# GpSimd's sums and differences written in pieces of half the width or less

## What is computed

```python
        x = x + jnp.einsum('bse,ed->bsd', mixed, w_out[l])
        h = rmsnorm(x, norm_mlp[l])
        u = jax.nn.relu(jnp.einsum('bsd,df->bsf', h, w_up[l]))
        x = x + jnp.einsum('bsf,fd->bsd', u * u, w_down[l])
```

## Time and profile before

| | |
|---|---|
| median of three timed runs | 2396.8 us (2395.7 to 2396.91) |
| the profiled execution | 2394.05 us, of which the span is 2392.4 us |
| TensorE matmul busy | 2326.6 us, 97% |
| VectorE busy | 1520.1 us, 64% |
| ScalarE busy | 1154.1 us, 48% |
| GpSimd busy | 706.9 us, 30%, 593 instructions |

### The profile page before, as it was taken

One profiled execution on the slowest core, in us unless ns is written; L12 is line 12 of the kernel. 1 busy time (PEld: TensorE's weight loads), 2 busy tenths in 40 slices (PEclk: granted clock), 3 DMA queues, 4 the chain that ended last, 5 costly groups with the idle time before them and its releaser, 6 DMA issues.

```text
span 2392.4 us, 34959 instructions
## 1 busy us (share of the span) xinstructions
PE 2326.6 (97%) x11346; PEld 1934.7 (81%) x11346; DVE 1520.1 (64%) x2623; ACT 1154.1 (48%) x2226; POOL 706.9 (30%) x593
## 2 busy tenths in 40 slices
PE   7999999999999998999899999999999999999998
PEld 5888888788888886887687877888888888888887
DVE  6588873688888886566745655444465555564454
ACT  5211112788888886223545555555553233333243
POOL 2000000111111114235568764666640032120132
PEclk9999999999999999999999999999999999999999
DMA  5567765666666565766455576654457486564464
GB/s 189 215 235 278 268 242 163 180 160 156 160 157 157 152 156 169 248 218 202 170 183 163 189 286 242 202 160 152 154 190 260 165 298 234 193 219 162 138 219 160
DMA packets 253970, 469.09 MB, mean 196 GB/s; under 512 B 59336, under 2 KB 119752, under 8 KB 246032
## 3 DMA queue, kind: packets, MB, share of 16 engines
q1 hardware_dynamic: 247808, 451.11, 58.6%
q0 software_dynamic: 6048, 16.52, 2.6%
HBM read 316.13 MB, written 151.42 MB: 195 GB/s over the span
## 4 chain that ended last, share of the span: by engine, by line
PE 51%; DVE 3%; POOL 2%; issue 2%; DMA 1%; ACT 1%; SPq 0%; POOLq 0%; ACTq 0%; DVEq 0%
PE m_ps L2533 24%; PE m_ps L2556 23%; PE m_ps L1685 4%; DMA b_kept<-f_kept 1%; POOL m_mix L1548 1%; DVE f_up_lo L2389 1%; PE m_ps L2574 0%; DVE m_xn L1653 0%; DVE m_xm L1646 0%; DVE m_mix L1622 0%; ACT m_mix_hi L1585 0%; DVE keep_lo L2408 0%; POOL h_raw L1560 0%; POOL f_kept L2157 0%; DVE hop_lo L1659 0%
## 5 line engine op out<-in xcount | busy, mean ns | idle before, releaser
L2556 PE MATMUL m_ps<-keep_hi,hop_hi 128*128 128x512 f32 x880 | 342.5, 389 | 0.4 <-DVE hop_lo L2392 0.4
L2556 PE MATMUL m_ps<-keep_hi,hop_lo 128*128 128x512 f32 x880 | 342.4, 389 | 0.0
L2556 PE MATMUL m_ps<-keep_lo,hop_hi 128*128 128x512 f32 x880 | 342.3, 389 | 0.0
L2392 DVE TENSOR_TENSOR hop_lo<-h_raw,hop_hi 128x512 fp32r<-128x512 f32 x224 | 176.6, 789 | 236.8 <-ACT hop_hi L2228 236.7
L2389 DVE TENSOR_TENSOR f_up_lo<-wide_raw,f_up_hi 128x512 fp32r<-128x512 f32 x160 | 182.5, 1142 | 223.0 <-ACT f_up_hi L2223 222.9
L2228 ACT ACTIVATE hop_hi<-h_raw 128x512 fp32r<-128x512 f32 x224 | 140.8, 630 | 334.4 <-PE m_ps L2556 330.5
L958 POOL DMA_DIRECT2D o_main<-a_o x63 | 36.5, 580 | 775.2 <-ACT a_o L1326 726.6
L599 PE MATMUL p_ps_o<-p_ht_lo,p_w_hi 128*128 128x512 f32 x576 | 224.5, 390 | 0.0
L2533 PE MATMUL m_ps<-keep_hi,f_up_hi 128*128 128x512 f32 x512 | 202.8, 396 | 6.1 <-DVE f_up_lo L2389 4.7
L2533 PE MATMUL m_ps<-keep_hi,f_up_lo 128*128 128x512 f32 x512 | 201.3, 393 | 0.0
L2533 PE MATMUL m_ps<-keep_lo,f_up_hi 128*128 128x512 f32 x512 | 199.4, 390 | 0.0
(11 more groups left out here) (246 smaller groups left out, 5779.8 us busy)
## 6 DMA issues: line engine op xcount, KB each, us to landing
h_raw<-u_ops SPq DMA_DIRECT2D x224, 256.0 KB, 4.2
wide_raw<-in_w_up SPq DMA_DIRECT2D x32, 1024.0 KB, 7.2
u_ops<-f_u SPq DMA_DIRECT2D x128, 256.0 KB, 4.3
wide_raw<-in_x SPq DMA_DIRECT2D x59, 512.0 KB, 4.0
u_ops<-f_us SPq DMA_DIRECT2D x96, 256.0 KB, 2.3
proj_hi<-p_o_hi SPq DMA_DIRECT2D x17, 1024.0 KB, 6.2
proj_lo<-p_o_lo SPq DMA_DIRECT2D x17, 1024.0 KB, 8.3
h_raw<-in_w_down SPq DMA_DIRECT2D x58, 256.0 KB, 3.9
```

The source lines that it names most:

```text
L2392: nc.vector.tensor_tensor(lo, a_raw[:, (m - UP) % A_RING], hi.bitcast(F32), ALU.subtract).then_inc(op_lo_done, 1)
L2556: last = nc.tensor.matmul(down_banks[b % 2][t][:], a[:, cols], w[j], start=(j == 0 and m == 0), stop=(j == FG - 1 and m == 2))
```

## The change

The operations and their operands stay. Those of 512 columns become two of 256, L1560 with 1024 columns becomes two of 512, L2143 with 1024 becomes four of 256, and L2128 with 2048 becomes eight of 256. Waits stand ahead of the first piece, and the last piece signals. In numbers: 6 more instructions at L1560, 128 in `mix_w`, 128 in `mix_u`, 7 in `mix_tokens`, 24 in `mix_rest`, 293 in all.

```diff
@@ mix_out: mix_tokens
-                nc.gpsimd.tensor_tensor(dst[:, k], a[:, k], b[:, k], ALU.subtract).then_inc(t_mixed, 1)
+                for m in range(k.start, k.stop):
+                    last = nc.gpsimd.tensor_tensor(dst[:, m], a[:, m], b[:, m], ALU.subtract)
+                last.then_inc(t_mixed, 1)
...
+    def combine(dst, a, b, op):
+
+        half = dst.shape[1] // 2
+        for cols in (slice(0, half), slice(half, 2 * half)):
+            last = nc.gpsimd.tensor_tensor(dst[:, cols], a[:, cols], b[:, cols], op)
+        return last
...
@@ mix_w, mix_u: eight lines of this form
-                nc.gpsimd.tensor_tensor(s1[:], a21, a22, ALU.add).then_inc(w_mixed, 1)
+                combine(s1[:], a21, a22, ALU.add).then_inc(w_mixed, 1)
...
@@ mix_tokens
-            nc.gpsimd.tensor_tensor(raw[:, 2], raw[:, 2], raw[:, 0], ALU.subtract).then_inc(t_mixed, 1)
+            for k in range(4):
+                last = combine(raw[:, 2, k], raw[:, 2, k], raw[:, 0, k], ALU.subtract)
+            last.then_inc(t_mixed, 1)
...
@@ mix_rest
-            nc.gpsimd.tensor_tensor(dst[:, k], a[:, k], b[:, k], ALU.subtract).then_inc(t_mixed, 1)
+            for m in range(k.start, k.stop):
+                last = combine(dst[:, m], a[:, m], b[:, m], ALU.subtract)
+            last.then_inc(t_mixed, 1)
```

More of the change, by code:

```diff
@@ L2089, in mix_w @@
                     pool.wait_ge(op_lo_done, (g - 1) * NP + 3)
-                nc.gpsimd.tensor_tensor(s2[:], s1[:], a11, ALU.subtract).then_inc(w_mixed, 1)
+                combine(s2[:], s1[:], a11, ALU.subtract).then_inc(w_mixed, 1)
             elif which == 3:
-                nc.gpsimd.tensor_tensor(a21, a11, a21, ALU.subtract).then_inc(w_mixed, 1)
+                combine(a21, a11, a21, ALU.subtract).then_inc(w_mixed, 1)
             else:
@@ L2095, in mix_w @@
                 pool.wait_ge(op_lo_done, g * NP + 4)
-                nc.gpsimd.tensor_tensor(a12, a12, s2[:], ALU.subtract).then_inc(w_mixed, 1)
+                combine(a12, a12, s2[:], ALU.subtract).then_inc(w_mixed, 1)
         return mix_w
@@ L2113, in mix_u @@
                 pool.wait_ge(us_out[0], 16 * g)
-            nc.gpsimd.tensor_tensor(us[0][:], u12[b][:], u22[b][:], ALU.add).then_inc(u_mixed, 1)
+            combine(us[0][:], u12[b][:], u22[b][:], ALU.add).then_inc(u_mixed, 1)
             pool.wait_ge(u_mixed, 4 * g + 1)
-            nc.gpsimd.tensor_tensor(u12[b][:], u11[b][:], u12[b][:], ALU.subtract).then_inc(u_mixed, 1)
+            combine(u12[b][:], u11[b][:], u12[b][:], ALU.subtract).then_inc(u_mixed, 1)
             if g:
                 pool.wait_ge(us_out[1], 16 * g)
-            nc.gpsimd.tensor_tensor(us[1][:], us[0][:], u11[b][:], ALU.subtract).then_inc(u_mixed, 1)
+            combine(us[1][:], us[0][:], u11[b][:], ALU.subtract).then_inc(u_mixed, 1)
             pool.wait_ge(u_mixed, 4 * g + 3)
@@ L2123, in mix_u @@
                 pool.wait_ge(us_out[2], 16 * g)
-            nc.gpsimd.tensor_tensor(us[2][:], u21[b][:], us[1][:], ALU.subtract).then_inc(u_mixed, 1)
+            combine(us[2][:], u21[b][:], us[1][:], ALU.subtract).then_inc(u_mixed, 1)
         def mix_tokens():
             pool.wait_ge(hop_lo_done, hop_count[0, 3])
-            nc.gpsimd.tensor_tensor(raw[:, 2], raw[:, 2], raw[:, 0], ALU.subtract).then_inc(t_mixed, 1)
+            for k in range(4):
+                last = combine(raw[:, 2, k], raw[:, 2, k], raw[:, 0, k], ALU.subtract)
+            last.then_inc(t_mixed, 1)
         def mix_rest(n, half):
```

## The result

The changed kernel takes 2405.6 us (median of six runs, 2404.7 to 2412.2); the kernel before took 2396.7 beside it (six runs, 2395.05 to 2398.8). The ratio is 1.0043, with a 95% interval of 1.003 to 1.0056: slower by more than the 0.2% that can be told, and in the forecast range. The profiled execution took 2405.08 us, its span 2403.4, against 2394.05 and 2392.4.

What follows compares the result with a forecast made beforehand. TensorE was taken as the bound, so only its waits count, most of them with GpSimd behind. Terms 1.4 - 0.1 + 1.6 + 2.7 + 1.6 - 1.1 + 3.5 = +9.6 us gave 2406.4 us, range 2399.5 to 2412.

Steps and rivals of the forecast that it cites:

- What a piece costs: On GpSimd: each added piece takes 0.15 us more; 293 pieces add 44 us, mostly in idle time.
- A: Head mix, tiles 8 to 13: six turns +0.9 us, halved first weight combinations behind them +0.5; together +1.4 us.
- B: Start of the up stage, L2128 in eight: product 4's wait goes, one longer wait comes at product 6; -0.1 us.
- Slow clock behind B: After the long wait at product 6, TensorE's clock falls to 0.57 for a stretch: +1.6 us.
- C: Group 4: GpSimd ends later, the token-sum store is issued later, TensorE's wait at 1258.49 grows: +2.7 us.
- Slow clock behind C: After group 4's wait, grown to 4.1 us, TensorE's clock falls here too: +1.6 us.
- D: Group 11: VectorE waits only one piece each for L2124 and L2092, so TensorE's wait nearly goes: -1.1 us.
- E: Groups 15 and 16: VectorE work goes ahead at seams, SyncE's loads of kept parts start late: +3.5 us.
- Rival 2: GpSimd keeps its turn over its own pieces, so only the pieces count: +4.5 us, 2401.3; chance 0.17.
- that the clock would not fall: Rival: TensorE's clock does not fall after the new waits; sum 9.6 - 3.2, 2403.2 us; chance 0.20.
- that groups 5 to 9 fill up: Rival: GpSimd becomes the bound in groups 5 to 9, 1 us more in each: 2411.4 us; chance 0.08.
- that nothing pays for the seams: Rival: seams free VectorE at no cost, waits at the up stage's start and group 11 shrink: -3.6 us, 2393.2; chance 0.10.

Runs made afterwards that it cites:

- a_alone: The kernel before with only the six token differences of the head mix (L1560) in halves; one profiled execution, 2395.88 us.
- b_alone: The kernel before with only the first token difference of group 0 (L2128) in eight pieces; one profiled execution, 2402.09 us.
- b_whole: The changed kernel with the first token difference of group 0 (L2128) again as one operation; 2403.7 us, ratio 1.0026.
- best: The kernel before with group 4's token-sum store and kept-part loads 4 and 5 issued earlier, halves only at L2096 of group 0 and in group 11; 2392.3 us, 0.9984.
- e_whole: The changed kernel with only the four result sums of group 15 in one piece each; 2406.0 us, ratio 1.004.
- c_whole: The changed kernel with GpSimd's operations of group 4 in one piece each; 2406.3 us, ratio 1.0035.
- e_quarter: The changed kernel with the four result sums of group 15 in quarters of 128 columns instead of halves; one execution, 2406.5 us.

## Why the prediction was right

The time (2405.6 for 2406.4) and the direction came out, and so did the mechanism. The forecast difference was 9.6 us; the medians differ by 9.0, the two profiled executions by 11.0. The terms, one by one:

- **What a piece costs, 0.15.** Right: 0.12 to 0.15 from two and four pieces, 0.15 a turn in a_alone. But GpSimd's own time was forecast to grow by 44 us from pieces alone, and grew by 70: the text named the waits at seams and left them out of that number.
- **A, +1.4.** Measured +1.35: 0.56 in four turns, 0.1 for the first weight combinations (forecast 0.5), and 0.68 ahead of the first of those turns, a stretch that has two more turns with L1560 and in which kernels without the pieces differ by 0.3 among themselves. The loop was sized right and the term behind it too large; that the sum came out is luck, as the gap is filled by 0.2 to 0.4 us ahead of the loop that no run explains.
- **B, -0.1.** Measured -0.95. ScalarE's signal came 4.5 us later against the tile, forecast 5.0: the eight pieces and VectorE's work among them took 8.93 us where 5.6 + 3.75 = 9.35 was counted. That is about half of the miss. The rest is the end of the chain, "ScalarE's two halves (2.01) then run to 1161.7, VectorE's two in the seams of L2085 and L2090 to 1163.9", and behind them the additions, which came another 0.3 to 0.4 us sooner. How much the halves of L2090 and L2092 matter there is shown by b_alone, where VectorE waits for whole operations: its signal is as early (4.4), and yet it comes to -0.11. That this is the number of the forecast is luck.
- **Slow clock behind B, +1.6.** Measured 1.64 (interval C less the wait at its end). b_whole shows that it is this wait's: with two waits of 3.60 and 0.88 the slow stretch lies before product 6 and interval C holds none.
- **C, +2.7.** Measured 2.59 of longer wait, 2.38 less without group 4's pieces. Right, with its chain: the store is issued 3.44 us later against product 6, of which 1.64 is the slow clock, so 1.80 by the pieces and their seams, forecast 1.8.
- **Slow clock behind C, +1.6.** Measured 2.71. The mechanism was right, the size was taken from one stretch of before. Of all terms this one was off most, though the same place cost 1.5 in two other kernels (below). It wasn't a pure loss either: without it group 11 waits 1.57 us longer.
- **D, -1.1.** Measured -0.84 with the change, -0.85 in best: VectorE's L2421 takes 3.45 us for 4.55, which is the 1.1 of the forecast, but it starts 0.26 later against the products, as the residual ahead of it (L2402) takes 1.08 us for 0.82.
- **E, +3.5.** Measured +3.83, and 3.1 for it alone. The first load of kept parts is issued 4.14 us later against group 11's wait. The slow clock there was costed at nothing; two products on, the difference is +0.02.

The errors of +1.1 (clock behind C), +0.3 (E) and +0.3 (D) against -0.85 (B) and -0.2 (C and A) leave 0.7; the unchanged front stages brought 0.6 more. That is the difference between the sum of 9.6 and the 11.0 us of span. The time came out better than the terms did, since their errors cancelled.

Two numbers of the forecast do not follow from its own. Rival 2 has 0.17, half of it on each side of 0.2%; then slower is 0.45 + 0.20 + 0.08 + 0.085 = 0.815 and same 0.15, not 0.78 and 0.19. And the sum counts 22 pieces (6 in A, 12 in C, 4 in E), so that 0.06 instead of 0.15 for each would make it 2.0 us smaller, not 1.5.

Of the rivals, that the clock would not fall is refuted by 0.50 to 0.54 behind the waits of 6.80 and 3.96 us; that GpSimd keeps its turn, by 8.93 us for eight pieces that need 5.7 at 2.85 for four; that groups 5 to 9 fill up, by the absence of any wait of TensorE between 1264 and 1388; and that nothing pays for the seams, by product 6, C and E.

The page SBUF — State Buffer of the Trainium skill, section Who interferes with whom, describes the exclusion that B and E rest on, and the trace agrees (8.93 against 5.7). The fixed cost that was worked out from the Trainium skill, GPSIMD Engine Reference, section 3.1, an estimate of 0.06 us a piece, is under what is measured here (0.12 to 0.15).

What stays open: why the slow stretch costs 1.6 us at one time and 2.7 at another. The traces hold more on this than two values. Intervals C and D less the wait at their end are 90.95 to 90.97 and 121.17 to 121.22 us wherever no slow stretch starts them, so what lies above the kernel before (90.97 and 121.21) is the clock:

| wait ahead of the slow stretch | lost behind it |
|---|---|
| product 6, 6.80 to 6.83 (e_whole, c_whole, changed kernel, e_quarter) | 1.54, 1.58, 1.64, 1.82 |
| product 6, 7.14 (b_alone) | 2.37 |
| group 4, 3.48 and 3.69 (e_quarter, b_whole) | 1.49, 1.55 |
| group 4, 3.96 and 3.98 (changed kernel, e_whole) | 2.71, 2.66 |

At each place the longer waits cost about 1 us more, but a wait of 6.80 cost less than one of 3.96 elsewhere, and each value is from one execution. No run varied one wait alone.

## What to carry to other kernels

Where two engines take turns at memory, as GpSimd and VectorE do here, cutting one's instructions does not make room: it hands the turn to the other. Before cutting, ask who waits for the engine that is cut, above all a queue that issues DMAs in order, and cut only where nobody does (group 11 here: 0.85 us). If the damage comes through a late DMA, moving that DMA up in its queue is worth more than the length of any instruction (10.0 us of difference became 0.7), but only as far as nothing urgent is passed: with all three loads in front the stores of results behind them came late, and TensorE waited 5.01 us for a copy that needed one of them.

## What the hardware showed beyond the forecast

TensorE's clock was not a matter of a single wait's length. It was full behind 1.58 us (c_whole, 1267) and near half behind 6.80 and 3.96; yet in c_whole it was 0.69 in the stretch behind a wait of 1.97 us, while the forecast could point to a wait of 2.34 at 1474 without an immediate fall (1.00 from 1475 to 1479; it was 0.66 from 1479 to 1484, behind the next wait of 1.98). A slow stretch cost nothing where TensorE had to wait again behind it (b_whole at 1163, the kept parts), and 1.5 to 2.7 us where it did not. So a few short waits in lost time can be cheaper than one long one: the eight pieces of L2128 left interval B as it was and cost 2.4 us of full clock behind it.
